# First RMSNorm of a decoder trunk: the low halves of the normalised input move from VectorE to GpSimd

## The reference, cut to what matters

```
def _rmsnorm(x, w):
    xf = x.astype(jnp.float32)
    xf = xf * lax.rsqrt(jnp.mean(xf * xf, axis=-1, keepdims=True) + NORM_EPS)
    return xf * w.astype(jnp.float32)
...
    h = _rmsnorm(x, norm_mix_pre)
    proj = jnp.einsum('bld,de->ble', h, w_in.astype(f32))
```

## Time and profile before

| | us |
|---|---|
| median of 3 runs | 2748.74 |
| the 3 runs | 2748.72, 2751.32, 2748.74 |
| the profiled execution's own time | 2750.22 |
| its span, from the first to the last instruction | 2748.3 |
| PE busy in the span | 2682.9 (98%) |
| DVE busy | 1786.0 (65%) |
| ACT busy | 1421.9 (52%) |
| POOL busy | 183.0 (7%) |

### The profile page before, as it was taken

How to read it: one execution, slowest core, us unless ns; L and a number is a source line. 1 busy time by engine, 2 the same in 40 slices (tenths; PEclk the granted TensorE clock), 3 DMA queues, 4 the chain that set the end, 5 groups by cost and what they waited for, 6 DMA issues and landing times.

```text
span 2748.3 us, 59421 instructions
## 1 busy us (share of the span) xinstructions
PE 2682.9 (98%) x22077; PEld 2624.0 (95%) x22077; DVE 1786.0 (65%) x3218; ACT 1421.9 (52%) x2285; POOL 183.0 (7%) x297
## 2 busy tenths in 40 slices
PE   6999999999999999999989999989999999999999
PEld 5999999999989999999989999989999999999989
DVE  7888888744478888888864444576543355554475
ACT  6667676643356655656644334454443344443363
POOL 0111111100101111111110000000000000000000
PEclk9999999999999999999999999999999999999999
DMA  4555555455556666665545556535554555555534
GB/s 171 178 170 163 178 173 168 154 189 178 180 188 215 202 208 205 204 216 197 199 166 172 179 172 206 168 120 176 166 169 162 167 161 168 168 169 167 166 131 159
DMA packets 135290, 484.22 MB, mean 176 GB/s; under 512 B 17249, under 2 KB 19697, under 8 KB 134081
## 3 DMA queue, kind: packets, MB, share of 16 engines
q1 hardware_dynamic: 114560, 410.88, 45.0%
q0 software_dynamic: 20672, 72.55, 8.3%
HBM read 449.58 MB, written 33.78 MB: 176 GB/s over the span
## 4 chain that ended last, share of the span: by engine, by line
PE 84%; DVE 9%; ACT 3%; issue 2%; DMA 1%; DVEq 0%; POOL 0%; ACTq 0%; POOLq 0%
PE acc L1669 25%; PE acc L1670 25%; PE acc L1671 25%; DVE w_lo L1024 2%; DVE ccv L1312 1%; ACT w_hi L508 1%; PE bank L1669 1%; PE bank L1670 1%; PE bank L1671 1%; PE bank L1855 1%; PE bank L1963 1%; PE bank L1950 1%; PE bank L1781 0%; PE bank L1872 0%; DVE x L1513 0%
## 5 line engine op out<-in xcount | busy, mean ns | idle before, releaser
L1024 DVE TENSOR_TENSOR w_lo<-raw,w_hi 128x1024 fp32r<-128x1024 f32 x772 | 936.9, 1223 | 586.9 <-ACT w_hi L508 582.7
L1669 PE MATMUL acc<-h_hi,w_hi 128*128 128x288 f32 x3872 | 1159.6, 299 | 12.4 <-DVE h_lo L1061 8.4
L1671 PE MATMUL acc<-h_hi,w_lo 128*128 128x288 f32 x3872 | 1143.1, 295 | 0.0
L1670 PE MATMUL acc<-h_lo,w_hi 128*128 128x288 f32 x3872 | 1140.8, 295 | 0.0
L508 ACT ACTIVATE w_hi<-raw 128x1024 fp32r<-128x1024 f32 x772 | 809.8, 1054 | 435.6 <-PE acc L1671 377.6
L1669 PEld LDWEIGHTS acc<-h_hi,w_hi 128*128 128x128 f32 x3872 | 728.6, 188 | 21.3 <-issue 7.4
L1670 PEld LDWEIGHTS acc<-h_lo,w_hi 128*128 128x128 f32 x3872 | 729.1, 188 | 2.8
L1671 PEld LDWEIGHTS acc<-h_hi,w_lo 128*128 128x128 f32 x3872 | 728.3, 188 | 0.0
L1669 PE MATMUL acc<-u_hi,w_hi 128*128 128x288 f32 x1024 | 303.4, 296 | 0.0
L1671 PE MATMUL acc<-u_hi,w_lo 128*128 128x288 f32 x1024 | 302.1, 295 | 0.0
L1670 PE MATMUL acc<-u_lo,w_hi 128*128 128x288 f32 x1024 | 301.4, 294 | 0.0
(11 more groups left out here) (415 smaller groups left out, 3535.1 us busy)
## 6 DMA issues: line engine op xcount, KB each, us to landing
raw<-in_w SPq DMA_DIRECT2D x772, 512.0 KB, 3.3
ht<-in_ht POOLq DMA_DIRECT2D x64, 256.0 KB, 4.1
out_ssm_s<-ht POOLq DMA_DIRECT2D x64, 256.0 KB, 3.9
cbc<-cum_d POOLq DMA_DIRECT2D x8, 1152.0 KB, 7.0
hs<-in_s POOLq DMA_DIRECT2D x16, 512.0 KB, 4.6
out_hg_s<-hsn POOLq DMA_DIRECT2D x16, 512.0 KB, 5.0
x_in<-in_x SPq DMA_DIRECT2D x4, 576.0 KB, 5.8
mixb<-bmb POOLq DMA_DIRECT2D x16, 144.0 KB, 2.0
```

What stands on the lines that cost most here:

```text
L1024: V.tensor_tensor(w_lo[:, k], raw[:, k], w_hi[:, k].bitcast(F32), ALU.subtract).then_inc(lo_done, 1)
L1669: M.matmul(out, w_hi[:, k, i], hi[:, kt0 + i, ::-1], start=first and i == 0, stop=False)
L1670: M.matmul(out, w_hi[:, k, i], lo[:, kt0 + i, ::-1], start=False, stop=False)
L1671: op = M.matmul(out, w_lo[:, k, i], hi[:, kt0 + i, ::-1], start=False, stop=last and i == SK - 1)
```

## The change

The eight subtractions of the first norm leave DVE's list and stand at the head of GpSimd's list, each behind the same semaphore, with the same operands and the same semaphore at its end.

```
@@ -1056,11 +1056,6 @@
                 V.scalar_tensor_tensor(hn32[:, t], x_in[:, t], cols[:, C_MIXPRE + t:C_MIXPRE + t + 1], x_rs[:, :],
                                        ALU.mult, ALU.mult).then_inc(n_xn, 1)
 
-        def normalised_lo(c):
-            dve.wait_ge(n_hi, c + 1)
-            V.tensor_tensor(h_lo[:, 2 * c:2 * c + 2], hn32[:, 2 * c:2 * c + 2, ::-1],
-                            h_hi[:, 2 * c:2 * c + 2].bitcast(F32), ALU.subtract).then_inc(n_lo, 1)
-
         dve.wait_ge(cst_land, 16)
         dve.wait_ge(n_add, 12)
         V.tensor_tensor(stack2, ident[:, 0:HD], ident[:, HD:2 * HD], ALU.add).then_inc(dt_stack, 1)
@@ -1070,7 +1065,6 @@
         for c in range(NC):
             if c + 1 < NC:
                 normalise(c + 1)
-            normalised_lo(c)
             if c in (2, 5):
                 split_lo(0, (c + 1) // 3)
 
@@ -2104,6 +2098,14 @@
                 return v.rearrange("a p b n -> (a p) b n")
             return v.rearrange("a p c b n -> (a p) c b n")
 
+        def normalised_lo(c):
+            pool.wait_ge(n_hi, c + 1)
+            nc.gpsimd.tensor_tensor(h_lo[:, 2 * c:2 * c + 2], hn32[:, 2 * c:2 * c + 2, ::-1],
+                                    h_hi[:, 2 * c:2 * c + 2].bitcast(F32), ALU.subtract).then_inc(n_lo, 1)
+
+        for c in range(NC):
+            normalised_lo(c)
+
         pool.wait_ge(hg_zero, 1)
         pool.dma_start(hs0[:, :, :], io["s0"][0]).then_inc(hg_s0, 16)
 
```

More of the change, by code:

```diff
@@ L1057, in normalise @@
                                        ALU.mult, ALU.mult).then_inc(n_xn, 1)
[L1059 to L1062, removed]
         dve.wait_ge(cst_land, 16)
```

## The result

The changed kernel takes 2757.51 us (median of 9 runs, 2754.9 to 2758.76) against 2749.88 for the kernel before in the same runs: +7.6 us, a ratio of 1.0027 with a 95% interval of 1.0016 to 1.0037. It is slower, and the median lies beyond the 5.5 us that were named as the bound. The stated range holds it. In us the interval is 4.4 to 10.2, so the time alone fits the forecast itself (+4.8) as well as the first rival (turns and a late clock, +8.0, 2756.7, chance 0.18); the trace decides for something close to that rival.

A forecast was written before the change was run, and what follows sets the result against it. PE bounds the kernel, waiting in the first norm on DVE's `h_lo`. Taking turns costs 3.5 + 0.8 + 0.5 = +4.8 us: 2748.7 + 4.8 = 2753.5 us, range 2745 to 2758.

The forecast's parts named there:

- the bound: Whole-kernel time: about 0.2%, 5.5 us, is what a measurement can tell from no change.
- The stated range: Whole-kernel time: from 2745 to 2758 us.
- the first rival: First norm: DVE and POOL alternate and PE's clock rises only at the dt product; +8.0, 2756.7 us, chance 0.18.
- Where the time is decided: First norm: PE's 8.4 us wait for `h_lo`; nothing afterwards absorbs a shift, so the end moves with the last `h_lo`.
- Turns against side by side: First norm: DVE and POOL exclude each other, +4.8 us, or run together, -3.2 us (2745.5, chance 0.34).
- The sum of the turns: First norm under full exclusion: 3.5 for slower subtractions, 0.8 for the last `h_hi`, 0.5 for lost overlap; +4.8 us.
- the forecast's own terms for that stretch: DVE's queue in the norm: POOL subtractions of 1.11 us replace 0.67 us each; lost overlap of DVE instructions adds 0.5.
- the last `h_hi` uncovered: End of the norm: POOL waits 0.68 us and two handovers for the last `h_hi`, formerly hidden; +0.8 us.
- with the clock as before: First norm: DVE and POOL alternate while PE's clock behaves as in the kernel before; +4.8 us, 2753.5, chance 0.42.
- "Same": Whole-kernel outcome: neither slower nor faster by over 5.5 us; chance 0.64.
- "slower": Whole-kernel outcome: slower by over 5.5 us, above 2754.2 us; chance 0.34.
- GpSimd's own list: Start of POOL's list: ISA row ends before 17.3, `hs0` load has 28 us of cover; moving them costs nothing.

The follow-up runs named there:

- The first experiment: The changed kernel with ScalarE writing the scale x_rs to PSUM, so each VectorE normalisation reads one SBUF operand: 2749.43 us, ratio 0.9999 to the kernel before.
- the third experiment: The changed kernel with 48 unread matmuls more on TensorE ahead of the waits for chunks 3 to 7: 2755.72 us, ratio 1.0022 to the kernel before.
- the last: Kernel before with scale in PSUM, subtractions of chunks 1, 3, 5 on GpSimd, 15 unread matmuls ahead of chunk 5's wait: 2746.16 us, ratio 0.9986.
- the run with VectorE first: The changed kernel with GpSimd's eight subtractions waiting until VectorE has made all 16 normalisations: 2757.98 us, ratio 1.0032 to the kernel before.

## Why the prediction was right and where it was wrong

**Where the time is decided: right.** The wait for `h_lo` was the only place; the shift of 7.27 us at the slab after the dt product is not absorbed (7.6 at the end). The sentence that the end gains or loses what the last `h_lo` does was too strong, though: the last `h_lo` lost 5.0, and the clock added 2.25 behind it.

**Turns against side by side: right.** Weighed 6 to 4 for turns from rows that could not decide it, and it was turns throughout. The first experiment shows that the operands are the reason: with one of them in PSUM the two engines run side by side. The rule of the Trainium skill (SBUF — State Buffer, "Who interferes with whom") thus agrees with the trace, with this number beside it: the blocked VectorE instruction loses 1.16 us of the 1.40 that the subtraction lasts, not all of them.

**The sum of the turns: right in total (4.8 forecast, 5.0 measured), in part by luck: two terms are wrong and cancel.** The subtraction was put at 1.11 us, in proportion to `hvbd`; by itself it takes 1.40. What counts in the queue, however, is the 1.16 for which it holds VectorE up, since it overlaps the VectorE instructions beside it by the other 0.24. Up to the last normalisation the queue changed by 7 x 1.16 - 6 x 0.67 = +4.1; the forecast's own terms for that stretch make 7 x 1.11 - 6 x 0.67 + 0.5 = +4.3. The tail (the last `h_hi` uncovered, then a subtraction of 1.40 alone) gave +0.7, where the forecast's terms make 1.11 + 0.8 - 2 x 0.67 = +0.6. The whole stretch began 0.18 later, which isn't the change's doing: in the other runs it begins between 16.9 and 17.2. The estimate from the Trainium skill (GPSIMD Engine Reference, section on elementwise cycle accounting) was 1.26: too low as well, though nearer to 1.40 than the proportion was.

**The clock: wrong, and this is the step that failed.** The forecast took the turns "with the clock as before" at 0.42 against 0.18 for a late clock. The argument against the rival was that PE had kept the high level through 25 to 32 with as many gaps. It counted the gaps, and the count didn't carry over. The windows of the kernel before, the whole stretch and then its emptiest part:

```profile
25.20:32.75 7.55, 4.97 (x30) 4.13 (x31) 7.37 (x18) 4.73 (x8) 0.00 (x0) 1.00 0.38 132
27.86:30.92 3.06, 1.06 (x6) 0.82 (x6) 3.01 (x5) 1.08 (x4) 0.00 (x0) 1.00 0.17 25
```

Over the whole PE is busier there (4.97 of 7.55 us) than in the changed kernel ahead of the fall (1.39 of 3.06). But a part of the same length with 1.06 us of work and a gap of 1.61 passed at 1.00. So neither the longest gap nor the busy share of one stretch tells the two kernels apart. That filling the gaps keeps the clock is shown (the third experiment and the last); which measure of the gaps decides stays open. The rival's form was off too: the clock did not rise late; it rose near 24.5 (in the kernel before between 23.91 and 25.45) and fell back. The run with half of the subtractions has the rival's form: 0.24 apart up to the dt product. Its price was put at 2.6 to 3.6 us and is 2.25 (0.74 + 1.51).

**The chances.** "Same" had 0.64 and "slower" 0.34. With the clock's 2.25 us the sum is 7.3, past 5.5; with the turns alone, 5.0, it would have been "same". Whether the median passed the bound hung on the clock.

**GpSimd's own list: right.** Its first subtraction starts at 18.89, 0.09 after the first `h_hi`; the ISA row was hidden, and the load of `hs0` went out at 38.68, 5 us later than before, without a wait behind it.

## What to carry to other kernels

Work that moves to a second engine is only won if the two can read at the same time: before moving an elementwise instruction from VectorE to GpSimd, count the SBUF operands of what will run beside it on VectorE; one operand in PSUM is enough to free it here. And where TensorE is fed in small pieces, a slower feeder can cost twice, as here: 5.0 us by its own delay and 2.25 by the clock that falls in the gaps. Where a change makes gaps on TensorE, a forecast needs a price for the low clock with a chance of its own; a high clock through earlier gaps does not rule it out. Where the gap can't be closed, unread matmuls can fill it: here 15 of them moved the dt product from 32.67 to 31.08.

## What the runs showed of the hardware that was not expected

Two SBUF operands are not the only case. In the first experiment POOL was still at work when VectorE came to the small instructions after the norm:

```profile
29.21 0.25 DVE L1074 RECIPROCAL lbm<-lbm 128x16 f32<-128x16 f32 x1
29.50 1.06 DVE L1076 TENSOR_TENSOR lbm<-lbm 128x16 f32<-128x16 f32 x1
30.59 1.34 DVE L1078 TENSOR_SCALAR lbc<-lbm 128x16 f32<-128x16 f32 x1
31.84 0.17 DVE L1079 TENSOR_SCALAR lbc<-lbm 128x16 f32<-128x16 f32 x1
```

A TENSOR_SCALAR with one SBUF operand of 16 elements took 1.34 us beside a subtraction and 0.17 as POOL ended (31.89), while a RECIPROCAL with one operand kept its 0.25. In the run with VectorE first two more of them took 1.35 and 1.40. The Trainium skill, SBUF — State Buffer, "Who interferes with whom", counts TENSOR_SCALAR among the instructions that can take the shared ports in a faster mode; these rows agree with that, though they show the blocking and not the mode. And the turns are strict: in the changed kernel, wherever the next subtraction had its input already (20.61, 22.20, 29.79 and 31.39), exactly one VectorE instruction ran before it, although more were ready; neither engine pushed the other aside.
